# The first modulation columns in the order 0, 2, 1, 3, VectorE's share ahead of the row scaling

## What is computed

```
mod = jnp.dot(jax.nn.silu(cond), w_ada) + b_ada           # cond: c_ctx for context, c for latent rows
sh1, sc1, gt1, sh2, sc2, gt2 = [m[:, None, :] for m in jnp.split(mod, 6, axis=-1)]
h = _rmsnorm(x, g_pre_mix) * (1 + sc1) + sh1
z = jnp.einsum('bld,de->ble', h, w_in)
```

## Time and profile before

| | us |
|---|---|
| median of three runs | 1750.72 (1750.28 to 1750.83) |
| span of the profiled execution | 1747.8 |
| TensorE matmuls busy in it | 1737.1 |
| VectorE busy | 1201.3 |
| ScalarE busy | 680.1 |
| GpSimd busy | 258.1 |

### The profile page before, as it was taken

One profiled execution on the slowest core, in us unless ns is written; L12 is line 12 of the kernel. 1 busy time (PEld: TensorE's weight loads), 2 busy tenths in 40 slices (PEclk: granted clock), 3 DMA queues, 4 the chain that ended last, 5 costly groups with the idle time before them and its releaser, 6 DMA issues.

```text
span 1747.8 us, 27002 instructions
## 1 busy us (share of the span) xinstructions
PE 1737.1 (99%) x10495; PEld 1633.9 (93%) x10495; DVE 1201.3 (69%) x2553; ACT 680.1 (39%) x1218; POOL 258.1 (15%) x255
## 2 busy tenths in 40 slices
PE   8999999999999999999999999999999999999998
PEld 3999999999999999999998899999999999888887
DVE  4786566457556654464455579888888888798998
ACT  3732221224144243262243454434344444444454
POOL 2010000100000000010000052434433333100000
PEclk9999999999999999999999999999999999999999
DMA  9233433434334454165242331233222222686877
GB/s 350 54 95 111 111 95 112 132 99 137 119 100 144 132 135 159 63 238 185 83 137 85 109 122 68 83 117 105 91 72 73 76 76 76 188 290 221 268 247 248
DMA packets 216275, 236.17 MB, mean 135 GB/s; under 512 B 11568, under 2 KB 160828, under 8 KB 216148
## 3 DMA queue, kind: packets, MB, share of 16 engines
q1 hardware_dynamic: 200916, 179.54, 33.7%
q0 software_dynamic: 10752, 38.00, 6.4%
q10 hardware_dynamic: 4480, 16.91, 2.4%
HBM read 181.49 MB, written 52.92 MB: 134 GB/s over the span
## 4 chain that ended last, share of the span: by engine, by line
PE 90%; DVE 5%; ACT 1%; issue 1%; POOL 1%; SPq 1%; DMA 1%; DVEq 0%; POOLq 0%; ACTq 0%
PE ps L1426 17%; PE ps L1083 13%; PE ps L1085 13%; PE ps L1084 13%; PE ps L1368 6%; PE ps L1443 5%; PE ps L1445 5%; PE ps L1444 5%; PE ps L1249 2%; PE ps L1251 2%; PE ps L1250 2%; PE ps L1233 2%; PE ps L1237 2%; PE ps L1235 2%; DVE mid_g L2603 1%; DVE up_lo L2124 1%
## 5 line engine op out<-in xcount | busy, mean ns | idle before, releaser
L1083 PE MATMUL ps<-H_hi,ring_hi 128*128 128x384 f32 x1224 | 415.4, 339 | 0.5 <-DVE H_lo L2124 0.2
L1085 PE MATMUL ps<-H_hi,ring_lo 128*128 128x384 f32 x1224 | 409.2, 334 | 0.0
L1084 PE MATMUL ps<-H_lo,ring_hi 128*128 128x384 f32 x1224 | 409.2, 334 | 0.0
L1083 PEld LDWEIGHTS ps<-H_hi,ring_hi 128*128 128x128 f32 x1224 | 229.9, 188 | 2.5 <-DVE H_lo L2124 1.8
L1084 PEld LDWEIGHTS ps<-H_lo,ring_hi 128*128 128x128 f32 x1224 | 230.0, 188 | 0.2
L1085 PEld LDWEIGHTS ps<-H_hi,ring_lo 128*128 128x128 f32 x1224 | 229.7, 188 | 0.0
L2311 DVE SCALAR_TENSOR_TENSOR Cst<-Cst,GE,ps 128x257 f32<-128x257 f32 x56 | 26.8, 478 | 167.4 <-PE ps L1237 167.4
L1426 PE MATMUL ps<-T_hi,up_hi 128*128 128x288 f32 x608 | 130.5, 296 | 0.3 <-ACT held_g L1959 0.3
L1426 PE MATMUL ps<-T_lo,up_hi 128*128 128x288 f32 x608 | 130.2, 296 | 0.0
L1426 PE MATMUL ps<-T_hi,up_lo 128*128 128x288 f32 x608 | 130.1, 296 | 0.0
L2124 DVE TENSOR_TENSOR up_lo<-up_raw,up_hi 128x512 fp32r<-128x512 f32 x114 | 88.4, 778 | 57.5 <-ACT up_hi L1917 57.5
(11 more groups left out here) (324 smaller groups left out, 3584.0 us busy)
## 6 DMA issues: line engine op xcount, KB each, us to landing
raw<-in_w_in_dram SPq DMA_DIRECT2D x44, 512.0 KB, 4.0
up_raw<-in_w_up_dram SPq DMA_DIRECT2D x38, 512.0 KB, 5.1
w_raw<-in_w_down_dram SPq DMA_DIRECT2D x66, 256.0 KB, 3.3
raw<-in_w_ada_dram SPq DMA_DIRECT2D x32, 512.0 KB, 5.3
X<-z_f SPq DMA_DIRECT2D x44, 256.0 KB, 3.9
GE<-z_gates SPq DMA_DIRECT2D x72, 128.0 KB, 4.0
w_sub<-in_w_down_dram SPq DMA_DIRECT2D x33, 256.0 KB, 4.0
z_w_diff<-w_raw SPq DMA_DIRECT2D x22, 256.0 KB, 2.7
```

The lines of the kernel that those rows point to most:

```text
L1083: pe.matmul(out, whi, xhi, start=first, stop=False)
L1084: pe.matmul(out, whi, xlo, start=False, stop=False)
L1085: return pe.matmul(out, wlo, xhi, start=False, stop=last)
```

## The change

The order of the groups becomes 0, 2, 1, 3 in the loads, in TensorE's rows and in ScalarE's row copies. Columns of group 1 are turned later, beside those of group 3, after the first product cell. TensorE does the group sum and the columns of 2 ahead of all rows of group 3, and the first half of the rows of 3 ahead of the four `first_norm`. VectorE multiplies its share of group 2 before it scales the rows of x.

```diff
+    ROW_ORDER = (0, 2, 1, 3)
-    ROW_BANK = (0, 1, 2, 1)
+    ROW_BANK = (0, 2, 1, 1)
             ada_load(0)
             x_load(0)
-            ada_load(1)
+            ada_load(DVE_GROUP)
...
-            ada_load(2)
+            ada_load(1)
             ada_load(3)
...
                 if g == 3 and k0 == 0:
-                    pe.wait_ge(row_read, 2)
+                    pe.wait_ge(row_read, ROW_ORDER.index(2) + 1)
...
             def ada_cols(g, at):
-                pe.wait_ge(row_read, g + 1)
+                pe.wait_ge(row_read, ROW_ORDER.index(g) + 1)
...
             ada_rows(0)
-            ada_rows(1)
             ada_rows(DVE_GROUP, 0, PE_CELLS, PE_CELLS)
             pe.wait_ge(vectors_in, 16 * 11)
...
+            ada_rows(1)
+            pe.wait_ge(vec_done, 2)
+            ada_cols(0, 0)
+            ada_group_sum()
+            ada_cols(DVE_GROUP, 2 * ADA0).then_inc(ada_used, ADA0 // 2)
+            ada_rows(3, 0, 4)
             pe.wait_ge(x_scaled, TB)
             for k in range(4):
                 first_norm(0, k)
-
-            pe.wait_ge(vec_done, 2)
-            ada_cols(0, 0)
-            ada_cols(1, 8)
-            ada_rows(3, 0, 4)
-            ada_group_sum()
-            ada_cols(DVE_GROUP, 2 * ADA0).then_inc(ada_used, ADA0 // 2)
             ada_rows(3, 4, KD)
...
                         if b == 0 and m == 0 and k == 1:
+                            ada_cols(1, 8)
                             ada_cols(3, 24).then_inc(ada_used, ADA0 // 2)
...
             def row_copy(n):
                 act.wait_ge(row_done, n + 1)
-                act.activation(ada_row[:, n, :], ps[0:2, ROW_BANK[n], :], ACT.Copy).then_inc(row_read, 1)
+                g = ROW_ORDER[n]
+                act.activation(ada_row[:, g, :], ps[0:2, ROW_BANK[g], :], ACT.Copy).then_inc(row_read, 1)
...
-            scale_x(0)
             dve.wait_ge(cond_done, 1)
             ada_group(PE_CELLS, KD)
+            scale_x(0)
             dve.wait_ge(vec_done, 2)
             first_coef(0)
```

## The result

| | before | changed |
|---|---|---|
| median, us | 1750.72 (7 runs, 1749.21 to 1751.01) | 1754.99 (7 runs, 1754.57 to 1757.42) |
| span of the profiled execution | 1747.8 | 1753.7 |
| first product cell in it | 37.50 | 42.98 |
| second coefficients in it | 39.09 | 44.37 |

The ratio is 1.0029, 95% interval 1.0019 to 1.0038: the changed kernel is slower, by 3.3 to 6.7 us (the medians differ by 4.3 us; the ratio makes 5.1 of it). In a later series, beside other runs of the kernel before with a median of 1750.54 us, it had a median of 1758.0 us (5 runs, ratio 1.0040, 1.0026 to 1.0053).

The account below looks back on a forecast made before the run. TensorE was taken to bound the kernel, with nothing behind the ramp hiding a shift: 3.8 us for its new order plus 1.7 us for a fallen clock made 5.5 us, from 1750.7 to 1756.2 us, range 1753.8 to 1758.0.

Parts of the forecast that it names:

- What bounds the kernel: Whole kernel: TensorE is busy 1737.1 of 1747.8 us, so any ramp shift passes to the end in full.
- The loads: Ramp: groups 1 and 2 swap landing times, group 2 at 16.43 us and group 1 at 23.15; no price by itself.
- The vectors: Ramp, before group 1's rows: packets pass at 18 to 19 us, so their three turns are done by about 19.6.
- the hole: TensorE before group 1's rows: some 3.5 us idle until 23.15, nearly 5 us counted from 18.2.
- VectorE's share first: VectorE in the ramp: share ends by 25.3 us, x scaled by 29.1; costs nothing.
- TensorE's new order: Ramp from 23.15 us: group 3 ends at 41.1 instead of 37.01, second coefficients at 42.9; loss 3.8 us at full clock.
- the sum: Ramp total: 3.8 us for TensorE's reordered work plus 1.7 us for its clock, 5.5 us.
- The clock: Group 1's first records: TensorE's clock level falls while idle and costs 1.7 us, bounds 0 and 3.4.
- The clock holds: Rival, ramp: idleness costs TensorE no clock level, loss only 3.8 us, time 1754.5 us; chance 0.22.
- low for longer: Rival, group 1's rows: two low stretches or most rows slow, loss 7.2 us, time 1757.9 us; chance 0.12.
- Span and median: Whole kernel: profiled span goes from 1747.8 to 1753.3 us; median stays 2.9 us above it, at 1756.2.

Follow-up runs that it names:

- the run with the old order: The changed kernel with VectorE scaling x before its share of group 2, as in the kernel before; median 1757.76 us, repeated at 1756.88 us.
- The run with the old loads: The changed kernel with only the loads put back to groups 0, 1, 2, 3; 1759.67 us, ratio 1.0051.
- the filled hole: The changed kernel with four extra warm-up-tile products into an unused bank, so TensorE is not idle between 18.2 and 23.3 us; median 1755.61 us.
- the kernel with VectorE on group 1: Load order 0, 2, 1, 3 kept, VectorE's share moved from group 2 to group 1, x scaled first; 1751.06 us, ratio 1.0004 to the kernel before.

## Why the prediction was right, and where it was off

- **What bounds the kernel.** Right in the main: a shift of 5.27 us at 46.7 us is 5.26 at 935.6 and 5.17 at 1514.6. That nothing behind the ramp changes it is not quite so: the same comparison for the changed kernel's second profile gives 8.57 us at 103.0 and at 935.6 us, 8.77 at 1629, and 8.32 from 1698 on.
- **The loads.** Right: group 2's first part started TensorE at 16.39 and group 1's at 23.30, where 16.43 and 23.15 were set.
- **The vectors.** Off: their turns were set at 19.6 and came at 21.31, since TensorE waited 3.04 us for the last vector. That the packets pass at 18 to 19 us did not mean that the semaphore was there. It moved no later work, as group 1 came later still; but the hole was split into 3.04 and 1.53 us, where 3.5 us in one piece had been set.
- **VectorE's share first.** Right: no effect, shown by the run with the old order. The share ended at 24.57 (25.3 at the latest), x was scaled at 27.22 (29.1).
- **TensorE's new order.** Right: the second half of group 3 ended at 42.68, less 1.36 for the clock 41.3, where 41.1 was worked out, and the first cell at 41.6 at full clock, where 41.5 was. Against 37.50 that is 4.1 us. The second coefficients stood at 44.37, less 1.36 is 43.0, set at 42.9: a loss of 3.9 us against the 3.8 of the sum.
- **The clock.** The mechanism was right, its size and its frame were not. The term was 1.7 us with bounds 0 and 3.4; the first profile had 1.36, the second 4.4, outside the bounds, because the level fell a second time behind the small products, which the sum did not consider. And the kernel before was taken to lose nothing, from one profile; in two others its ramp is 1.3 us later. These two errors have opposite signs. The medians differ by 4.3 us in the first series and by 7.5 us in the second, and the forecast of 5.5 lies between: that it came so near is in part luck. "The clock holds" would have been the nearer number for the first series (1754.5 against 1754.99), and "low for longer" for the second (1757.9 against 1758.0); but the first is not what happened, since the clock held in neither profile.
- **Span and median.** 2.9 us were put around the span; the profiled execution of the changed kernel took 1755.46 us with a span of 1753.7, so 1.8 lies around it. By that the profiled execution of before took 1749.6 us, below its median of 1750.72. The span itself, set at 1753.3, came out at 1753.7; 0.6 us of it is the late part below, which the sum did not have.

The Trainium skill ("TensorE: Matmul & The Clock Gate", Part 1: The HAM clock gate) traces the lower level to idleness and its end to sustained activity. The run with the old loads bears that out (7.00 us idle, then 3.58 us for four records), and the filled hole does for its half. That the level also falls where the matmul records show no idle time, as behind the group sum in the filled-hole run, stands in these traces beside that rule; the runs do not settle what makes it fall there, nor why it does in one execution and not in the next.

**Left open:** the further 0.6 us arise at one place of the changed kernel's first profile, where TensorE waits for VectorE:

```profile
1655.96 0.50 PE L1443 MATMUL ps<-B_hi,A_hi 128*128 128x512 f32 x1 [0.42 <-DVE A_lo L2125]
```

Between 1629 and 1698 us the same comparison moves by +0.6 us there, by -0.45 in the changed kernel's second profile, by +0.2 and -0.4 in the two repeats of the kernel before, and by +1.2 in the filled hole. Since it moves both ways without the change, nothing says that the 0.6 us belong to the change; no run addressed what moves it.

## What to carry to other kernels

When an order is changed so that a result comes earlier, count for the engine on the path how much of its work can still begin before each transfer lands: here the group with the first half's scale landed earlier, but 16 large records that had filled the time of a transfer now stood behind it, and an advance on VectorE of 6.6 us was worth nothing. A swap of loads wants a swap of shares with it, as the kernel with VectorE on group 1 shows. And before a few microseconds are argued from one profile, take a second one: the same ramp moved by 1.3 us in the kernel before and by 3 us in the changed one, nearly all of it by the clock.

## What the runs showed of the hardware that was not expected

- TensorE lost its level without an idle stretch: in the filled-hole run from 30.23 to 32.98 it did 24 small records back to back, and the next eight took 4.96 us instead of 3.60. The changed kernel's first profile shows the same products without a fall. In the one profile with all of group 2 on TensorE, which has no group sum, the level held too; a single profile does not show that the sum is the cause.
- The records of group 1 brought the level back themselves: after 3 to 7 of them 0.85 us apart, the spacing was 0.43 again, so the longest of the rivals (low for most of the rows of 1) came close in the second profile, with 2.70 us on group 1 alone.
- VectorE's tiny operation of two inputs from SBUF was held by GpSimd as the large cast is: 1.99 us in the changed kernel, from 34.81 to 36.80, where GpSimd's operation ends at 36.77:

```profile
34.44 2.33 POOL L934 TENSOR_TENSOR ring_lo<-raw,ring_hi 128x1024 fp32r<-128x1024 f32 x1 [27.16 <-ACT ring_hi L1566]
...
34.81 1.99 DVE L2166 SCALAR_TENSOR_TENSOR coefA<-modT,vT 128x8 f32<-128x8 f32 x1
...
44.65 0.17 DVE L2166 SCALAR_TENSOR_TENSOR coefA<-modT,vT 128x8 f32<-128x8 f32 x1
```

  The same operation takes 0.17 us when GpSimd is idle. The Trainium skill ("SBUF — State Buffer", SBUF: two separate sides) calls the shared pair of ports a lock that is held for a whole instruction, against VectorE's operations with two inputs in SBUF too if GpSimd's operation reads SBUF, as this one does (`raw`, `ring_hi`); the trace agrees. It did no harm here, as ScalarE waited for the turned x until 38.34.
